# A fused mixer and mixture-of-experts layer on one core: attention products turned round, the expert loop shifted, and the last stage's rows loaded early

## What is computed

```python
h = rms_norm(x, norm1_g) * (1 + scale1) + shift1
u, v_a, q, k, v_b, gates = jnp.split(h @ w_in, PROJ_SPLITS, axis=-1)
out_a = chunk_spatial_gate(gelu(u), layer_norm(gelu(v_a), ln_v_g, ln_v_b))
p = sink_softmax(s, sink)                       # s: window of 128, scores of 8 heads
o = jnp.einsum('bnhgqk,bnkhd->bnqhgd', p, vv)   # 2 key/value heads, 4 query heads on each
merged = g_a * (out_a @ w_pa) + g_b * (out_b @ w_pb)
x = x + gate1 * (merged @ w_o)
h2 = rms_norm(x, norm2_g) * (1 + scale2) + shift2
idx, wts = hier_route(h2, w_rg, b_rg, w_re, b_re)     # 2 of 32 experts for each token
y = routed_experts(h2, idx, wts, w_gate, w_up, w_down)
x = x + gate2 * y
y_prompt = rms_norm(x, normf_g)
```

## Time and profile before

| | us |
|---|---|
| median of 3 runs (2252.49 to 2255.87) | 2255.22 |
| the profiled execution's own time | 2261.7 |
| its span, first to last instruction | 2260.1 |

### The profile page before, as it was taken

The page is one execution under the profiler, slowest core; times in us unless marked ns, Lnnn a source line. Parts: engine busy times, 40 slices in busy tenths (PEclk is TensorE's granted clock), DMA queues, the critical chain, the costliest instruction groups (busy, mean ns, idle before and its releaser), DMA issues. The chain is left out here.

```text
span 2260.1 us, 30494 instructions
## 1 busy us (share of the span) xinstructions
PE 1931.8 (85%) x9577; PEld 1502.8 (66%) x9578; DVE 1094.1 (48%) x1912; ACT 759.3 (34%) x1323; POOL 269.8 (12%) x334
## 2 busy tenths in 40 slices
PE   6699999999869999996599999991799999999600
PEld 2588888888647777773488888860566666666400
DVE  3466666666330000012355555553566666666558
ACT  2244444444130000002212112110466666666512
POOL 0000000000000000000000101001122222222213
PEclk9799999999779999998799999995799999999855
DMA  8321222222084454534544433412987454999187
GB/s 282 122 87 74 87 86 95 95 94 78 22 307 182 178 193 166 205 112 171 180 149 148 149 130 139 145 63 62 320 299 263 162 192 141 310 306 307 35 334 290
DMA packets 196410, 381.98 MB, mean 169 GB/s; under 512 B 46174, under 2 KB 125534, under 8 KB 190178
## 3 DMA queue, kind: packets, MB, share of 16 engines
q1 hardware_dynamic: 156532, 304.92, 38.9%
q0 software_dynamic: 21936, 59.40, 7.0%
q10 hardware_dynamic: 17904, 17.19, 2.5%
HBM read 297.10 MB, written 104.26 MB: 178 GB/s over the span
## 5 line engine op out<-in xcount | busy, mean ns | idle before, releaser
L2011 DVE TENSOR_TENSOR gate_up_lo<-expert_ring,gate_up_hi 128x2048 fp32r<-128x2048 f32 x106 | 238.2, 2289 | 162.3 <-ACT gate_up_hi L1942 162.3
L1942 ACT CAST gate_up_hi<-expert_ring 128x2048 fp32r x106 | 196.6, 1902 | 159.8 <-issue 122.0
L260 PE MATMUL mix<-w_mix_hi,hT_hi 128*128 128x512 f32 (+3 forms) x544 | 203.8, 375 | 3.8 <-DVE hT_lo L640 2.6
L262 PE MATMUL mix<-w_mix_lo,hT_hi 128*128 128x512 f32 (+3 forms) x544 | 198.7, 365 | 0.0
L261 PE MATMUL mix<-w_mix_hi,hT_lo 128*128 128x512 f32 (+3 forms) x544 | 198.4, 365 | 0.0
L2081 PE MATMUL ex<-expert_ring,hidden_T 128*128 x400 | 181.8, 597 | 8.8 <-issue 8.6
L1150 DVE SCALAR_TENSOR_TENSOR ma_rows<-tanh_rows,ga 128x512 f32<-128x512 f32 (+1 forms) x34 | 21.8, 683 | 340.5 <-PE ga L262 190.1
L260 PE MATMUL ex<-gate_up_hi,gathered_T_hi 128*128 128x512 f32 x408 | 165.4, 405 | 6.1 <-DVE gathered_T_lo L2002 6.1
L262 PE MATMUL ex<-gate_up_lo,gathered_T_hi 128*128 128x512 f32 x408 | 161.0, 394 | 0.0
L261 PE MATMUL ex<-gate_up_hi,gathered_T_lo 128*128 128x512 f32 x408 | 160.5, 393 | 0.0
L260 PE MATMUL gb<-w_b_hi,h_parts_b 128*128 128x512 f32 (+1 forms) x272 | 109.7, 403 | 28.7 <-DVE w_b_lo L1449 18.9
(11 more groups left out here) (295 smaller groups left out, 3813.4 us busy)
## 6 DMA issues: line engine op xcount, KB each, us to landing
expert_ring<-in_w_gate SPq DMA_DIRECT2D x32, 1024.0 KB, 6.1
expert_ring<-in_w_up SPq DMA_DIRECT2D x32, 1024.0 KB, 8.6
expert_ring<-in_w_down SPq DMA_DIRECT2D x32, 1024.0 KB, 10.3
h_parts<-hT_split SPq DMA_DIRECT2D x16, 1024.0 KB
mixer_parts<-oT_split SPq DMA_DIRECT2D x32, 512.0 KB
w_ada_part<-in_w_ada SPq DMA_DIRECT2D x16, 1024.0 KB, 10.7
h_parts_b<-hT_split SPq DMA_DIRECT2D x16, 1024.0 KB
expert_pairs<-weighted_rows ACTq DMA_DIRECT2D x16, 1024.0 KB, 8.0
```

Source lines behind the costliest of these rows:

```text
L260: nc_mm(out, left[0], right[0], start=first, stop=False)
L262: return nc_mm(out, left[0], right[1], start=False, stop=last)
L1942: nc.scalar.copy(wg[par][0][:, n * HG:(n + 1) * HG], w[:, bass.ds(slot * GU + n * HG, HG)]).then_inc(w_hi, 1)
L2011: nc.vector.tensor_tensor(wg[par][1][:, at], w[:, bass.ds(slot * GU + n * HG, HG)], wg[par][0][:, at].bitcast(F32), ALU.subtract).then_inc ...
```

## The change

1. **Mixers.** The probability-value products are turned round: the values (64 columns) are the weights, and four heads' transposed probabilities (128x512) stream past. Four products take the place of 16; those of key/value head 0 write PSUM partitions 0 to 63 of a bank, those of head 1 partitions 64 to 127 of the same bank. The result comes out already transposed, so the four transposes of `ob` and DVE's `out_b` go. The division by the softmax sum moves ahead of the transposes, onto the probabilities: a DVE multiply of 128x2048 in `sums`. PE's order changes: the 16 transposes stand behind the v projection, the products in the middle of the u projection. ACT takes `gelu_v` ahead of the copies and `keep_v` behind `back_out`; DVE takes its copies inside `norm_v` and `norm` ahead of `low_b`. The sample rows' copies and the row order of `w_pb` follow the new layout of heads.
2. **Experts.** Each loop turn takes the steps 2p and 2p+1 instead of 2p+1 and 2p+2, so that the step behind the last block is gone; the last block's transposes, down products, weighting and scatter stand behind the loop (`rest`). The block list has a fifth row with that number. ACT makes the weighting between the two halves of the weights' high part.
3. **Residual rows and gates.** The expert ring stays allocated during `combine`. When the last experts' gate/up weights are used, SP loads the residual rows of tiles 0 to 7 into ring slots 0 and 2 and the three constant rows into slot 1, still in `experts`. `combine` waits for no constant, loads residual rows only from tile 8 on, eight tiles ahead, and its SP and DVE loops are written out.

```diff
@@ sweep_mixers, ACT and DVE @@
             def back_out(i):
-                act.wait_ge(ob_turned, i + 1)
+                act.wait_ge(pv_done, i + 1)
...
-                nc.scalar.copy(obT[:, 0, :], ps[5][:, :]).then_inc(obT_hi, 1)
+                nc.scalar.copy(obT[:, 0, :], ps[4][:, :]).then_inc(obT_hi, 1)
...
+                nc.vector.tensor_tensor(sc[:, :, :], sc[:, :, :], tiny[:, 48:56].unsqueeze(2).to_broadcast([P, NH, 2 * P]),
+                                        ALU.mult).then_inc(weighed, 1)
...
-            def out_b(i):
-                dve.wait_ge(pv_done, i + 1)
-                nc.vector.tensor_tensor(ob[:, :].rearrange("p (h d) -> p h d", d=HD), ps[4][:, :].rearrange("p (h d) -> p h d", d=HD),
-                                        tiny[:, 48:56].unsqueeze(2).to_broadcast([P, NH, HD]), ALU.mult).then_inc(ob_ready, 1)
@@ sweep_mixers, PE @@
-                    for h in range(NH):
-                        g = h // NC
-                        for j in range(2):
-                            last = nc.tensor.matmul(ps[4][:, h * HD:(h + 1) * HD], pT[:, 2 * h + j, :],
-                                                    vv[:, j, g * HD:(g + 1) * HD], start=(j == 0), stop=(j == 1))
...
-                project(2, 0, 512, m, range(0, 2))
+                project(2, 0, 512, m, range(0, 4))
                 if not first:
-                    pe.wait_ge(ob_ready, i)
-                    for k in range(4):
-                        last = turn(ps[5][:, k * P:(k + 1) * P], ob[:, k * P:(k + 1) * P])
-                    last.then_inc(ob_turned, 1)
-                project(2, 0, 512, m, range(2, KD)).then_inc(u_done, 1)
+                    pe.wait_ge(pT_a, i)
+                    pe.wait_ge(pT_d, i)
+                    pe.wait_ge(v_moved, i * 2)
+                    for j in range(2):
+                        for g in range(NKV):
+                            heads = pT[:, 2 * NC * g:2 * NC * (g + 1), :].rearrange("p (h j) q -> p h j q", j=2)[:, :, j, :]
+                            last = nc.tensor.matmul(ps[4][g * HD:(g + 1) * HD, :].rearrange("p (h q) -> p h q", h=NC),
+                                                    vv[:, j, g * HD:(g + 1) * HD], heads, start=(j == 0), stop=(j == 1))
+                    last.then_inc(pv_done, 1)
+                project(2, 0, 512, m, range(4, KD)).then_inc(u_done, 1)
@@ sweep_gate_a, SP @@
+            for c in range(NC):
+                sp.wait_ge(raw_lo, KD + 4 + c - 3)
+                for g in range(NKV):
+                    h = g * NC + c
+                    sp.dma_start(raw[c][g * HD:(g + 1) * HD], a["w_pb"][0, h * HD:(h + 1) * HD, :]).then_inc(raw_in[c], 16)
@@ experts, SP: behind the last loads of down weights @@
+            x1, gates = late_rows(w)
+            for n, e in ((0, NE - 4), (1, NE - 2)):
+                wait_apart(sp, w_lo, last_block(e) * 2, passed)
+                for k in range(4):
+                    at = 4 * n + k
+                    sp.dma_start(x1(at, P), s["x1"][at * P:(at + 1) * P, :]).then_inc(x1_in, 16)
+                if n == 0:
+                    wait_apart(sp, w_lo, last_block(NE - 3) * 2, passed)
...
+            sp.wait_ge(gates_in, 48)
+            sp.wait_ge(x1_in, 128)
@@ experts, ACT: in a step, and behind the loop @@
-                weights(b + 2, par)
+                weights(b + 2, par, (0,))
                 weigh(b - 1, (slot - 1) % 4, landed, before)
+                weights(b + 2, par, (1,))
                 records(b + 1, (slot + 1) % 4)
...
+            rest = listed(act, 4, 0)
+            records(rest * 2 + 1, LAST)
+            hidden(rest * 2 + 1, 1)
+            weigh(rest * 2 + 1, LAST, 16, rest * 16)
@@ experts, PE @@
             step(1, 1, 1)
-            step(2, 0, 1)
             with pe.Fori(1, PAIRS) as p:
                 with pe.If(p * 2 < total):
+                    step(p * 2, 0, p)
                     step(p * 2 + 1, 1, p + 1)
-                    step(p * 2 + 2, 0, p + 1)
+            rest = listed(pe, 4, 0)
+            turn_h(rest * 2 + 1, 1)
+            out(rest * 2 + 1, 1)
@@ combine, SP and DVE @@
+            def load(i, m):
+                sp.wait_ge(summed, i - NX + 1)
+                sp.dma_start(x(i, m), s["x1"][i * P:i * P + m, :]).then_inc(x_in[i % NX], 16)
...
-            dve.wait_ge(const_in, 16 * 3)
...
-                dve.wait_ge(x_in[k], n * 16 + 16)
+                if i >= NX:
+                    dve.wait_ge(x_in[i % NX], i // NX * 16)
```

More of the change, by code:

```diff
@@ L580, in tile @@
                 values(i, P, first)
+                gelu_v(i, P)
                 if not first:
                     back_probs(i - 1)
-                gelu_v(i, P)
-                keep_v(i, first)
                 turned(i, P, first)
@@ L591, in tile @@
                     back_out(i - 1)
+                keep_v(i, first)
                 gelu_u(i, P, first)
@@ L758, in tile @@
                 keys(i, P, c)
-                if not first:
-                    back_probs(i - 1)
-                norm_v(i, P, c, None if first else lambda: out_b(i - 1))
+                norm_v(i, P, c, None if first else lambda: back_probs(i - 1))
+                norm(i + 1, m_next, g_next)
                 if not first:
                     low_b(i - 1)
-                norm(i + 1, m_next, g_next)
                 out_a(i, P, bs)
@@ L1800, in experts @@
         QUADS = MAX_BLOCKS // 4
+        LAST = 4
+        half = lambda slot: 1 if slot == LAST else slot % 2
         weight = lambda slot: rec[:, slot, 1:2].bitcast(F32)
@@ L1954, in weigh @@
                 if before is not None:
[L1955 removed]
+                    act.wait_ge(stored[half(slot)], before)
                 act.wait_ge(rec_in[slot], landed)
                 for n in range(2):
[L1958 removed]
+                    last = nc.scalar.activation(y[:, half(slot), n * 512:(n + 1) * 512], ps[5 + n][:, :], ACT.Copy, scale=weight(slot))
                 last.then_inc(y_out, 1)
```

153 lines of the change are left out of this document (67 added, 86 removed).

## The result

The changed kernel takes **2193.95 us** (median of 4 runs, 2190.60 to 2195.41) against 2255.55 us before (4 runs, 2252.49 to 2258.23): ratio 0.9725, 95% interval 0.9708 to 0.9743, 61.6 us less. Measured again in a later session it took 2190.84 against 2257.20, ratio 0.9709 (0.9689 to 0.9729). Some 12 to 16 us came from a place that the forecast had put at nothing: the steps of the expert loop.

What follows compares the result with a forecast made beforehand. PE was taken to bound mixers and expert loop, DVE and DMA the combination. Gains of 31 + 15.4 + 0.5 - 0.4 = 46.5 us from 2255.2 gave 2208.7 us; own range 2199 to 2214, 8-in-10 range 2197 to 2226.

Steps and rivals of the forecast that it cites:

- Mixers: Mixer tiles: 1.9 us less on PE in each of 16 tiles, 31 us in all (6 to 35).
- The 2.0: Mixers: the four new value products take 2.0 us a tile, with two column halves side by side (1.8 to 3.54).
- The rule of the Trainium skill: Mixers: column halves would wait for each other's loads, for a sum of 22 to 34 us, not 46.5; 7%.
- Who may be late: Mixers: DVE's multiply is covered with 2.5 us to spare, its copies out of PSUM with 0.3 us.
- the numbered rivals: Five alternatives: halves queue up 8%, loads between rounds 7%, DVE's copies late 18%, combination stays on DMA 10%, slower 2%.
- The split weights: Expert loop: they cost nothing; DVE gets the second half 1.3 us later, a whole step before PE wants it.
- Gathers of the same stretch have a step of lead: Expert loop, beside the early loads: gathers there have one step to spare; no size given.
- The window that I took as the step's measure: Last third of the expert loop: PE busy 30.00 of 30.00 us, and a step takes 9.9 us.
- Drain: End of the expert loop: one step goes, but only 0.5 us is gained (-1 to +3).
- Combination: Last stage: first add 5.5 us in rather than 20.9, a gain of 15.4 us (10 to 20).
- I leave all: Combination: all 4.6 us of DVE's waits for stores stay, since the DMA engines are full.
- Gate sweeps and block list: Four more SP transfers in the gate sweep cost nothing (0 to 1 us); two DVE steps for the list, +0.4 us.

Runs made afterwards that it cites:

- gather_late: The changed kernel with two fills of 128x1024 on POOL between each scatter and the next gather; 20.9 us more than the changed kernel.
- old_loop_early_pairs: The changed kernel with the loop's old form and the first two pairs of expert rows loaded during POOL's drain; 2183.52 us, ratio 0.9670.

## Why the prediction was right and wrong

**Mixers: right, 34.4 us rather than 31.** A tile gives 2.15 us instead of 1.9: the products took 1.87 us, not 2.0, and the removed work was 4.0 us by difference, not 3.9. The 2.0 rested on the right rows with a wrong reading: I took whole halves to run side by side, and it is the two passes of one narrow product. That both readings give the same sum was luck. The rule of the Trainium skill that I set against it ("TensorE: Matmul & The Clock Gate", Part 3, The mechanism) says that loads overlap a running product only where the row group differs. By the rows of this case that would have cost 12 to 24 us. In this trace the rounds start 0.43 to 0.48 us apart, and the loads of the second product begin 0.06 us into the passes of the first, on the same rows. So the trace disagrees with that sentence. The same section names loads into a background weight buffer as another case; no run here can tell whether these are such loads.

**Who may be late: right, and close.** The copies ended 0.37 us ahead, forecast 0.3, and the run with one more copy shows that 0.2 of it was real. The multiply took 2.29 us under cover. None of the numbered rivals came.

**The split weights "cost the loop nothing": the step that failed.** It is true as a cost, but the split was a gain of 12.3 (undone) to 15.9 us (alone), put at nothing in the sum. The step looked at who waits for the second half (DVE, then PE a step later) and not at what the earlier weighting lets go: scatter, then gather, then PE's transposes and list reads. "Gathers of the same stretch have a step of lead" was wrong. A gather issued 7.2 us into a step has 7.3 us until the 4.5 us mark of the next and takes a median of 7.5 to land, so in 19 of 47 steps the lead was gone. The window that I took as the step's measure lies at 2090, among the last six steps, which all took 10.0 us; the loop's sum, 514.3 us over 49 steps, would have shown it. Nor could any of the forecast's bounds have made up for it: all gains at their high bounds give 2197.6 us, still above the measured time. That 2208.7 less the 14.8 us of the loop is 2193.9, just what was measured, is partly luck, since other terms moved too.

**Drain: 0.5 us forecast, -0.6 measured, within its bounds.** The order of events came as worked out, with a longer stand: PE had next to no work for 7.8 us (4 to 6 forecast), then down products of 6.27 us instead of 3.60, with a mean granted clock of 0.59 of full between 2074.80 and 2081.10 (1.00 with the old form). What was missed is that the split, kept with the old form, shortens the end by 2.4 us (37.9 to 35.5), and the shift gives that and 0.6 more back. Without the split the shift's one profile has an end of 36.4 us, 1.5 shorter than before, but its median is only 0.7 lower, which can't be told from 0.

**Combination: 15.4 forecast, 16.5 measured alone, 20.1 in the first pair of profiles.** The first add, 5.5 us forecast, came at 5.55. The 4.6 us of store waits, of which the forecast said "I leave all", were a mis-sized term, though a small one: with the rows loaded early 0 to 0.2 us are left, in nine profiles with this last stage. But the 4.6 us were also one execution's, the highest of seven.

**Gate sweeps and block list.** The gate sweeps, put at 0 to 1 us more, took 402.3 to 402.6 and 489.3 to 491.1 us, against 402.4 to 404.1 and 490.5 to 490.8 before. From their end to the first expert product it was 45.6 and 45.9 us, against 47.0 twice before, where 0.4 more was forecast; why is not known.

**Three slips in the working, without effect on the forecast.** The mixers' upper bound of 35 us is 33.6 by its own terms, (3.9 - 1.8) x 16, and the measured 34.4 lies above it. The low end of the forecast's own range, 2199, is 2197.6 by its terms. And 14 us of loads from 2088.84 on end near 2103, not 2108, which leaves 25 us of cover.

**The whole.** 34.4 + 14.8 + 20.1 - 0.6 = 68.7 of the 71.3 us between the first two profiles. Alone, the mixers give 36.1, the split 15.9, the last stage 16.5, the shift 0.7 (not told from 0). The first three make 68.5, and the kernel that has them without the shift is 70.0 below the kernel before. With the shift it is 61.6 and 66.4 below in two sessions, so what the shift costs is known only to a few us.

## What to carry to other kernels

When an operation moves forward on one engine, follow what its result releases through every queue to the bound engine, even if the move was made for something else: here 16 us hung on a gather that stood in POOL's queue behind a scatter. Take a loop's time from all its steps, not from a quiet window, and see what a sequencer still has to do behind a wait. Removing a useless last turn gained nothing here, since ACT set the end and PE, left idle, came back at the low clock. And when a run delays something by putting work in front of it, look at what that work itself disturbs: in `gather_late` it made 9 of 23.5 us.

## What the runs showed of the hardware

**List reads slow down beside work on POOL.** Reading a block's list entry from SBUF into a register takes 0.3 us, but just after an indirect gather is issued it took up to six times that. These are the reads of ACT, PE and DVE, first before the change and then in the changed kernel (durations min/median/max in ns, then the first and last start in us, then a count of one form):

```profile
L1807 ACTq TENSOR_LOAD <-block_lists x215: 273/283/1806, 1578.8 to 2128.9; - x108
...
L1807 PEldq TENSOR_LOAD <-block_lists x101: 295/303/496, 1600.3 to 2122.9; - x101
...
L1807 DVEq TENSOR_LOAD <-block_lists x54: 302/342/1836, 1578.8 to 2126.6; - x54
```

```profile
L1807 ACTq TENSOR_LOAD <-block_lists x262: 272/279/947, 1541.9 to 2073.1; - x131
...
L1807 PEldq TENSOR_LOAD <-block_lists x102: 296/305/1269, 1562.5 to 2069.9; - x102
...
L1807 DVEq TENSOR_LOAD <-block_lists x53: 301/307/766, 1541.9 to 2064.8; - x53
```

From block 2 on, of the 75 reads that began within 1 us of a gather's issue before the change, 41 took over 0.6 us; of 42 in the second microsecond 11, of 31 in the third 4, and of those later none. Of 81 reads that began within 2 us of a scatter's issue and away from a gather, none did. It is not the gather's alone: in `gather_late` 33 of the 36 slow reads go with two plain fills on POOL, while of 107 reads that overlapped a gather there only 2 were slow. What on POOL does it, and when, is not shown.

**Narrow float32 products.** A float32 product with 64 stationary columns and 512 moving ones costs 0.43 to 0.53 us here, its two passes together (four of them 1.87 us), where the whole-array one costs 0.86.

**POOL's drain.** Between the last scatter's landing and the next stage POOL drains for 8.4 to 8.6 us in every kernel here. It does not hold other queues: 2 MB that SP issued at its start (2083.47 in `old_loop_early_pairs`) landed by 2090.70, while the drain ran to 2092.01.
